# Steps 30 to 18 of each half's block inversion on VectorE, steps 17 to 1 on GpSimd

## What is computed

```python
def rwkv7_scan(r, w, k, v, a, bvec, state):
    def step(s, inp):
        r_t, w_t, k_t, v_t, a_t, b_t = inp
        sa = jnp.einsum('bhvk,bhk->bhv', s, a_t)
        s = s * w_t[:, :, None, :] + sa[..., None] * b_t[:, :, None, :] + v_t[..., None] * k_t[:, :, None, :]
        return s, jnp.einsum('bhvk,bhk->bhv', s, r_t)
```

## Time and profile before

| what | value |
|---|---|
| median of 3 runs | 3740.5 us (3738.04 to 3743.9) |
| the profiled execution | 3744.43 us, span 3742.6 us |
| PE busy | 2679.9 us (72%) |
| DVE busy | 1692.2 us (45%) |
| POOL busy | 782.7 us (21%) |
| ACT busy | 794.9 us (21%) |
| the 240 products and 240 additions of the inversion on POOL | 120.9 and 126.5 us |

### The profile page before, as it was taken

One profiled execution on the slowest core, in us unless ns is written; L12 is line 12 of the kernel. 1 busy time (PEld: TensorE's weight loads), 2 busy tenths in 40 slices (PEclk: granted clock), 3 DMA queues, 4 the chain that ended last, 5 costly groups with the idle time before them and its releaser, 6 DMA issues. The chain is left out here.

```text
span 3742.6 us, 47858 instructions
## 1 busy us (share of the span) xinstructions
PE 2679.9 (72%) x19670; PEld 2170.2 (58%) x19670; DVE 1692.2 (45%) x2430; ACT 794.9 (21%) x1269; POOL 782.7 (21%) x734
## 2 busy tenths in 40 slices
PE   4999973214788763543487789889239797979698
PEld 2788871004677651533433667668239797979343
DVE  3466005673355634958724435435423434344221
ACT  1111112211222112314101222222123232222000
POOL 1111110003556530504223111101002121212012
PEclk7999996557798875766798899999669898989899
DMA  5333223243333313011052232332260303120600
GB/s 217 140 127 95 89 70 108 86 126 113 81 89 101 97 26 94 0 41 32 7 192 64 79 92 98 93 103 82 33 113 13 125 17 120 41 96 1 247 34 28
DMA packets 299607, 319.27 MB, mean 85 GB/s; under 512 B 122355, under 2 KB 251838, under 8 KB 296598
## 3 DMA queue, kind: packets, MB, share of 16 engines
q1 hardware_dynamic: 273600, 312.70, 26.8%
q10 hardware_dynamic: 25814, 3.77, 0.6%
HBM read 203.69 MB, written 112.64 MB: 85 GB/s over the span
## 5 line engine op out<-in xcount | busy, mean ns | idle before, releaser
L1899 PE MATMUL PS<-w_out,y_in 128*128 128x512 f32 x832 | 361.0, 597 | 60.4 <-DMA y_in<-yT_d 34.9
L2434 PE MATMUL PS<-Q,K 128*128 128x128 f32 x2560 | 308.8, 285 | 125.0 <-PEq L109 71.6
L2434 PEld LDWEIGHTS PS<-Q,K 128*128 128x128 f32 x2560 | 305.6, 201 | 127.0 <-issue 127.0
L1899 PEld LDWEIGHTS PS<-w_out,y_in 128*128 128x128 f32 x832 | 159.4, 192 | 261.2 <-issue 200.0
L2518 POOL TENSOR_TENSOR weights_lo<-weights,weights_hi 128x1664 fp32r<-128x1664 f32 x32 | 120.2, 3756 | 733.3 <-ACT weights_hi L2495 733.3
L375 PE MATMUL PS<-hT_hi,w_in_hi 128*128 128x512 f32 (+1 forms) x640 | 242.3, 379 | 0.0
L2466 PE MATMUL PS<-V_hi,weights_hi 128*128 128x258 f32 x832 | 238.0, 286 | 4.0 <-DVE H L2574 4.0
L376 PE MATMUL PS<-hT_lo,w_in_hi 128*128 128x512 f32 (+1 forms) x640 | 238.7, 373 | 0.0
L377 PE MATMUL PS<-hT_hi,w_in_lo 128*128 128x512 f32 (+1 forms) x640 | 238.6, 373 | 0.0
L2468 PE MATMUL PS<-V_hi,weights_lo 128*128 128x258 f32 x832 | 234.8, 282 | 0.0
L2467 PE MATMUL PS<-V_lo,weights_hi 128*128 128x258 f32 x832 | 234.4, 282 | 0.0
(11 more groups left out here) (364 smaller groups left out, 5495.9 us busy)
## 6 DMA issues: line engine op xcount, KB each, us to landing
chunk_in<-in_d SPq DMA_DIRECT2D x40, 512.0 KB, 3.4
w_in<-in_e_w_in_dram SPq DMA_DIRECT2D x30, 512.0 KB, 4.8
xnew<-in_o_w_in_dram SPq DMA_DIRECT2D x30, 512.0 KB, 5.4
K<-k_d SPq DMA_DIRECT2D x20, 640.0 KB, 6.2
modw<-in_mod_w_dram SPq DMA_DIRECT2D x8, 1536.0 KB, 19.2
xnat<-in_mod_w_dram SPq DMA_DIRECT2D x8, 1536.0 KB, 8.3
v_d<-xnew SPq DMA_DIRECT2D x16, 640.0 KB, 3.0
k_d<-xc SPq DMA_DIRECT2D x16, 640.0 KB, 3.1
```

The source lines that it names most:

```text
L1899: last = pe.matmul(PS[:, 2 * (n % 4) + h, :], y[:, k, n * P:(n + 1) * P], w[:, k, 512 * h:512 * h + 512], start=(k == 0), stop=(k == n_k - 1))
L2434: last = pe.matmul(PS[:, 4 + n % 4, (j - j0) * P:(j - j0 + 1) * P], K[:, kt, j * P:(j + 1) * P], Q[:, kt, i * P:(i + 1) * P], start=(kt == ...
```

## The change

POOL now starts at step 17. The copy, the memset and steps 30 to 18 of a half are on DVE, in a function `invert(n, ks)`. For half 0 all thirteen steps stand in one piece in score_stage(1), behind the first chunk's rk. For half n+1 they stand in use_stage(n) in three pieces, each ahead of an eviction: steps 30 to 27 ahead of out(0), steps 26 to 23 ahead of out(1), steps 22 to 18 ahead of out(2). The last addition signals `half_inv`, for which POOL waits. The wait for `rel_in` moves from POOL to DVE.

```diff
+SHARED = 18
...
                 for n in range(HALVES):
-                    pool.wait_ge(s["rel_in"], 32 * (n + 1))
-                    step.link(pool.tensor_copy(U[64:104], Ut[64:104].rearrange("b s t -> b t s")))
-                    step.link(pool.memset(U[:].rearrange("b s t -> b (s t)")[0:104, 0:32 * 32:33], 1.0))
-                    for k in range(30, 0, -1):
+                    pool.wait_ge(s["half_inv"], n + 1)
+                    for k in range(SHARED - 1, 0, -1):
...
+                def invert(n, ks):
+                    if ks[0] == 30:
+                        dve.wait_ge(s["rel_in"], 32 * (n + 1))
+                        step.link(dve.tensor_copy(U[64:104], Ut[64:104].rearrange("b s t -> b t s")))
+                        step.link(dve.memset(U[:].rearrange("b s t -> b (s t)")[0:104, 0:32 * 32:33], 1.0))
+                    for k in ks:
+                        w = 31 - k
+                        prod = tmp[0:104, 0:k * w].rearrange("b (i j) -> b i j", i=k)
+                        step.link(dve.tensor_tensor(prod, U[0:104, 0:k, k:k + 1].broadcast_to([104, k, w]),
+                                                    U[0:104, k:k + 1, k + 1:32].broadcast_to([104, k, w]), ALU.mult))
+                        ins = dve.tensor_tensor(U[0:104, 0:k, k + 1:32], U[0:104, 0:k, k + 1:32], prod, ALU.add)
+                        if k > SHARED:
+                            step.link(ins)
+                        else:
+                            ins.then_inc(s["half_inv"], 1)
...
                         rk(m)
+                        if n == 1 and j == 0:
+                            invert(0, range(30, SHARED - 1, -1))
...
                     for j, m in enumerate(half_chunks(n)):
+                        if n + 1 < HALVES and j < 3:
+                            invert(n + 1, (range(30, 26, -1), range(26, 22, -1), range(22, SHARED - 1, -1))[j])
                         out(m)
```

More of the change, by code:

```diff
@@ L902, in rwkv_units @@
                 "d32_ps d32_sb t32_ps t32_sb y64_ps y64_sb t64_ps t64_dve t64_act wu_ps wu_sb out_ps out_dve out_act "
-                "ch_ps ch_sb rd_ps rd_sb mn_ps mn_sb sq_ok vr_ps vr_sb fin st gb_in step inv_step")
+                "ch_ps ch_sb rd_ps rd_sb mn_ps mn_sb sq_ok vr_ps vr_sb fin st gb_in step inv_step half_inv")
         def chunk(m):
```

## The result

The changed kernel takes 3771.66 us (median of 4 runs, 3765.57 to 3774.74), the kernel before 3739.27 us beside it (3734.13 to 3743.9): the ratio is 1.0085, with a 95% interval of 1.0065 to 1.0105. That is 32 us slower, where 28 were forecast (3768.8 against 3740.5).

What follows compares the result with a forecast made beforehand. The loop from y32 through the next half's inversion and SP's DMAs was taken as the bound; 35.1 us lost over seven distances, 6.8 gained before them: 28.3 slower, median 3768.8 us, range 3755 to 3794.

Steps and rivals of the forecast that it cites:

- What bounds the stage: From one half's y32 to the next: blocks land, POOL inverts for 37.4 us, SP's DMAs take 11.65, except with finals.
- The price of the steps: Copy, memset and steps 30 to 18 on DVE: 10.6 us per inversion against POOL's 17.4.
- (a): Links for free: each of 26 DVE instructions 0.12 us cheaper, kernel +9 us, 3750; chance 0.06.
- (c): Dearer steps: small strided, broadcast rows cost POOL's price on DVE, +28 to +82 us, halfway 3795; chance 0.15.
- Half 0: DVE is free before the first blocks land, so the first y32 starts at 937.1, 6.8 us earlier.
- Plain halves: Halves 1 and 2: DVE's last piece ends 29.7 us after y32 starts; distance to next y32 61.35 us.
- Halves with readouts: Halves 3, 5, 7: DVE's last piece ends 31.05 us after y32 starts; distance to next y32 62.7 us.
- Halves with finals: Halves 4 and 6: DVE's last piece ends 41.5 us after y32 starts; distance to next y32 73.65 us.
- SP's 11.65 us: SP's stores and reads back, from the end of POOL's steps to the next y32, taken as 11.65 us in each half.
- sum of 458.1: The seven distances between y32 starts, first to last half: 458.1 us against 423.0 before, 35.1 lost.
- rival (b): PE at full clock in readout stages if y32 doesn't wait in halves 4 and 6: +23 us, 3763; chance 0.17.
- Rival (d): Pieces vanish into DVE's waits for PE: with free steps 21 us faster, 3720; chance 0.04.

Runs made afterwards that it cites:

- half 0 alone: Against the changed kernel, only half 0 keeps its copy, memset and steps 30 to 18 on DVE; POOL does halves 1 to 7: 0.9984 of the kernel before.
- the gate: Half 0 as in the changed kernel; POOL does halves 1 to 7, starting each only after DVE evicted the previous half's t64: 1.0052 of the kernel before.
- the last two experiments: Against the changed kernel: thirteen steps placed ahead of y64, t64, out(0) in halves 1 to 7, 0.9985 of the kernel before; DVE steps fitted to each half's slack, 0.9924.
- the run in one piece: Against the changed kernel, halves 1 to 7 have all thirteen DVE steps together ahead of out(0): 1.0003 of the kernel before.
- the run with the pieces in DVE's waits: Against the changed kernel, halves 1 to 7 have the thirteen DVE steps ahead of y64, t64 and out(0): 0.9985 of the kernel before.

## Why the prediction was right

- **What bounds the stage.** The loop from y32 over the inversion and SP's DMAs to the next y32 was the bound, but for the halves with finals. Of the two runs with no DVE steps in halves 1 to 7, the one with half 0 alone left it at 422.5 us, and in the other a delay of 3.5 to 7.4 us at its start (the gate) put 25 us onto it.
- **The price of the steps.** 10.6 us worked out from the rows of other DVE instructions, 10.5 measured; the product of 234 elements takes 0.404 us, as forecast (0.40). The copy was 1.05 against 1.25. So (a), links for free, fell: from 902.00 to the next start at 902.44 pass 0.44 us for a 0.40 us instruction. The forecast set that against the Trainium skill (VectorE: DVE Perf Modes, "The DRAIN you can't avoid"), which measured the same time for copies with a semaphore after each and with one behind the last. Its 0.12 us were read from evictions that don't need each other's results; no run here has this chain without its links, so what a link costs in it isn't shown, and the rule isn't refuted. And (c), dearer steps, fell: small rows with strides and a broadcast operand cost what the rate of the earlier trace rows gives, 0.02 us more at 30 elements.
- **Half 0.** 6.8 us forecast, 7.2 measured (88.8 to 81.6), and 6.0 with half 0 alone. Of the 7.2, 0.7 are that the blocks landed earlier in this execution (39.05 us after the stage's start against 39.77).
- **Plain halves.** Forecast handover X + 29.7; the two measured are 963.21 - 934.89 = 28.3 and 1024.61 - 995.23 = 29.4. In the first PE delivered for out(0) 1.3 us earlier than in the earlier trace rows; its granted clock in the 17 us behind X(0) was 0.60, behind X(1) 0.50. The forecast had taken PE's delivery from the use stage of half 1 for both.
- **Halves with readouts.** Forecast 31.05, measured 31.5, 30.9, 30.95.
- **Halves with finals.** Forecast 41.5, measured 39.8 and 41.3. The bound beside it, 72.5 for DVE and PE alone, has a slip: two finals without POOL are 2 x 1.1 = 2.2 us shorter and not 1.8, so it is 72.1; it set no term of the sum. The final with POOL idle took 6.0 us, as forecast from the earlier trace rows: in the timeline of DVE, use_stage(3), its product shows 0.69 in place of the 0.95 of the earlier trace rows.

```profile
1139.97 3.34 DVE L1495 RECIPROCAL y_square<-y_square 128x512 f32<-128x512 f32 x1
1143.35 0.69 DVE L1496 TENSOR_TENSOR y_centered<-y_centered,y_square 128x512 f32<-128x512 f32 x1
```

- **SP's 11.65 us** were 11.7 to 11.9 in six halves, and 12.85 and 12.4 in halves 4 and 5. The first makes up for most of the early handover there (39.8), the second is why the distance from X(4) to X(5) is 63.5 and not 62.7. The forecast took the value from half 0 alone; in halves 2, 3 and 5 of the kernel before it was 12.7 to 13.0, so that the small value held was not worked out. All this is why the sum of 458.1 agrees to the decimal. The agreement of the sum is luck to about 2 us; that of its terms is not.
- **PE's clock**, rival (b). In halves 4 and 6 y32 waited for 1.97 and 0.99 us, and the last readout ended 17.7 us after X in both, where it had ended after 14.8 and, in use_stage(6), 14.2. The granted clock behind X(4) was 0.70 (this stretch of the trace of after), where the earlier trace rows have 1.00 for the same use stage. So PE was 2.9 and 3.5 us later there than without the new waits, and (b), which needed y32 not to wait, didn't come in. That the wait alone lowers the clock isn't shown: in the run in one piece y32 of halves 4 and 6 didn't wait, and the clock in the 17 us behind it was 0.90, with 0.66 in a stretch of 5 us (1191 to 1196); in the run with the pieces in DVE's waits it was 0.80 and 0.89.

```profile
1193.10:1210.00 16.90, 15.56 (x381) 14.53 (x383) 4.43 (x7) 4.48 (x10) 0.00 (x0) 0.70 0.18 40
```

- **Rival (d)**, faster, named the right condition: what counts is when the last piece ends. It isn't reached by cheaper steps but by another place, as the last two experiments show.
- **A sentence of the forecast that was too simple.** It laid the loss to two causes, the late start and the work between pieces, without a share for each. Measured one by one they don't add up in a plain way: the late start alone costs 25 us when POOL does all the steps (the gate), and the work between the pieces is 23 of the 35 when DVE does thirteen of them (one piece). The 12 us that stay lost in one piece are for the most part neither: they are PE and DVE's own chain, pushed back by the piece. The forecast's "6.4 to 20 us later" for taking up the blocks was too wide as well; by the traces it is 5 to 11 us (X + 13.7 to 18.3 against X + 7.3 to 8.6).

## What to carry to other kernels

A step that is moved to a faster engine gets that engine's queue too. Work out the time of the handover, that is the point at which the new engine takes up the data plus all that stands between the pieces, and compare it with the same point of before; only then does the speed of the steps count. Look too at whether anything waits for the result there: once the consumer doesn't, the moved steps lengthen the new engine's own chain. Filling an engine's idle time pays where it lies ahead of the work that others wait for: the same thirteen steps on the same engine made the kernel 32 us slower, no slower, or 6 us faster, by their place alone. And how much a half may take depends on the half: look for each pass of the loop how long the consumer waits for the result.

## What the runs showed of the hardware

- A linked small VectorE tensor_tensor on 104 partitions took 0.20 us at 30 elements and 0.40 at 234 (1.0 ns an element), and the next one started 0.03 to 0.04 us after its end. The same on GpSimd took 0.25 at 30 and 0.62 at 238: GpSimd loses little on the short ones. Strides and a broadcast operand made next to no difference on VectorE (0.404 us at 234 elements, where the rate of plain shapes in the earlier trace rows gives 0.396).
- VectorE's transposing copy of 40x1024 elements took 1.05 us, GpSimd's 1.93.
- Behind new waits of 2.0 and 1.0 us ahead of a burst of small matmuls the granted clock was 0.70 in the 17 us that followed, in both halves, against 1.00 before (the earlier trace rows for half 4). Without such a wait, but with other gaps in PE's work, it was 0.80 to 0.90 there in two other runs, so the wait isn't the only thing that counts.
